# One of four weight-block sums of a gate/up stage moved from an accumulating transfer to VectorE

## The reference

```
D_FF = 5632
hn = rmsnorm(h, ffn_norm_g[i])
h = h + (jax.nn.silu(hn @ w_gate[i]) * (hn @ w_up[i])) @ w_down[i]
```

## Time and profile before

| what | value |
|---|---|
| three runs, median | 2647.73 us (2647.01 to 2650.66) |
| the profiled execution's own time | 2634.65 us |
| its span, first to last instruction | 2633.1 us |
| mean granted TensorE clock | 0.997 |
| share of the span busy: PE, DVE, ACT, POOL | 98%, 62%, 44%, 13% |
| gate/up stage | about 1074 to 1942 us of the span, 44 pairs |

### The profile page before, as it was taken

How to read it: one execution, slowest core, us unless ns; L and a number is a source line. 1 busy time by engine, 2 the same in 40 slices (tenths; PEclk the granted TensorE clock), 3 DMA queues, 4 the chain that set the end, 5 groups by cost and what they waited for, 6 DMA issues and landing times.

```text
span 2633.1 us, 43908 instructions
## 1 busy us (share of the span) xinstructions
PE 2584.3 (98%) x16270; PEld 2098.3 (80%) x16270; DVE 1620.0 (62%) x2509; ACT 1166.1 (44%) x1680; POOL 353.6 (13%) x551
## 2 busy tenths in 40 slices
PE   8999999999999999899999999999999999999998
PEld 6786777777777678788888888888887888888887
DVE  6653563663663434988989889898873333334443
ACT  6535634644644434655555555555542222233321
POOL 3000110110110100211111111111141000001100
PEclk9999999999999999999999999999999999999999
DMA  5231232132222524877777877877777445333532
GB/s 175 80 89 61 64 97 61 64 91 66 73 75 72 169 84 136 233 229 203 225 220 206 228 204 218 226 205 228 207 240 278 123 156 177 107 94 99 182 120 74
DMA packets 147813, 391.06 MB, mean 149 GB/s; under 512 B 39625, under 2 KB 43209, under 8 KB 147689
## 3 DMA queue, kind: packets, MB, share of 16 engines
q1 hardware_dynamic: 114288, 273.85, 32.8%
q0 software_dynamic: 33408, 115.62, 16.8%
HBM read 344.78 MB, written 44.63 MB: 148 GB/s over the span
## 4 chain that ended last, share of the span: by engine, by line
PE 82%; DVE 7%; DMA 4%; ACT 4%; issue 2%; SPq 1%; POOL 0%; DVEq 0%; ACTq 0%; POOLq 0%
PE bank L1419 21%; PE bank L360 15%; PE bank L357 14%; PE bank L361 14%; PE bank L1421 10%; PE bank L398 4%; DMA raw<-w_down 1%; DMA squares_scratch<-sq_x 1%; ACT w_hi L345 1%; PE bank L523 1%; DVE w_lo L352 1%; DMA raw<-w_mix 1%; PE bank L552 1%; PE bank L539 1%; DVE w_lo L1381 0%
## 5 line engine op out<-in xcount | busy, mean ns | idle before, releaser
L352 DVE TENSOR_TENSOR w_lo<-raw,w_hi 128x1024 fp32r<-128x1024 f32 (+2 forms) x308 | 330.7, 1076 | 428.4 <-ACT w_hi L345 426.9
L345 ACT ACTIVATE w_hi<-raw 128x1024 fp32r<-128x1024 f32 (+2 forms) x308 | 284.7, 926 | 516.9 <-PE bank L361 388.3
L1419 PE MATMUL bank<-x_a,w_hi 128*128 128x512 f32 x1408 | 493.0, 394 | 4.1 <-issue 2.3
L357 PE MATMUL bank<-in_hi,w_hi 128*128 128x512 f32 x1088 | 455.2, 418 | 18.7 <-DVE in_lo L2123 11.0
L360 PE MATMUL bank<-in_lo,w_hi 128*128 128x512 f32 x1088 | 440.6, 405 | 0.0
L361 PE MATMUL bank<-in_hi,w_lo 128*128 128x512 f32 x1088 | 427.8, 393 | 0.0
L1421 PE MATMUL bank<-x_a,w_lo 128*128 128x256 f32 x1408 | 390.1, 277 | 0.0
L1419 PE MATMUL bank<-x_c,w_hi 128*128 128x512 f32 x1056 | 372.9, 396 | 2.6 <-DVE x_c L1305 2.6
L1419 PEld LDWEIGHTS bank<-x_a,w_hi 128*128 128x128 f32 x1408 | 264.0, 188 | 66.7 <-issue 2.8
L1421 PE MATMUL bank<-x_c,w_lo 128*128 128x256 f32 x1056 | 293.8, 278 | 0.0
L357 PE MATMUL bank<-act_hi,w_hi 128*128 128x512 f32 x704 | 274.5, 390 | 2.1 <-DVE h_t L2194 2.1
(11 more groups left out here) (309 smaller groups left out, 3846.1 us busy)
## 6 DMA issues: line engine op xcount, KB each, us to landing
raw<-w_mix SPq DMA_DIRECT2D x116, 512.0 KB, 3.9
raw<-w_gu SPq DMA_DIRECT2D x111, 512.0 KB, 6.9
raw<-w_down SPq DMA_DIRECT2D x64, 384.0 KB, 3.1
sum<-w_gu SPq DMA_DIRECT2D x43, 512.0 KB, 5.2
sum<-w_gu POOLq DMA_DIRECT2D x43, 512.0 KB, 8.0
raw<-w_down SPq DMA_DIRECT2D x64, 320.0 KB, 2.9
raw<-ple_gate SPq DMA_DIRECT2D x32, 512.0 KB, 3.8
raw_odd<-w_gu SPq DMA_DIRECT2D x22, 512.0 KB, 6.9
```

The lines of the kernel that those rows point to most:

```text
L345: nc.scalar.activation(w_hi[:, ring_slots(par2, half), 0:cols[half]], raw[:, half, 0:cols[half]], ACT.Copy).then_inc(hi_ready, 1)
L352: nc.vector.tensor_tensor(w_lo[:, s, 0:cols[half]], raw[:, half, 0:cols[half]], w_hi[:, s, 0:cols[half]].bitcast(F32), ALU.subtract).then_ ...
L357: nc.tensor.matmul(out, w_h, x_hi, start=start, stop=False, skip_group_check=True)
L1419: nc.tensor.matmul(by_half(bank[:]), w_h, both[:, :, i, :], start=opens[j] and i == 0, stop=False, skip_group_check=True)
```

## The change

`sum_1` of pairs 2 to 43 is now a DVE instruction, added in place: SP still loads `a21` into `sum_1`, and DVE adds the `a22` that is loaded for block 6 anyway. It stands in DVE's order at the start of step 2 of the pair before, ahead of the subtract of block 6. The accumulating transfer of `sum_1` is gone from POOL, with its 512 KB of traffic; that of `sum_3` stays. SP's wait for `sum_1` of the pair before is now a wait for DVE. The counts of `sum_ready` and of the POOL semaphores are adapted.

```diff
     def sum_done(p, k):
         if isinstance(p, int) and p == 0:
             return sum_ready, k
-        if isinstance(p, int) and p == 1 and k == 1:
-            return sum_ready, 5
-        return ((S("moved_0"), SQUARES_BACK[0] + 16 * (p - 1)), (sum_ready, 2 * p + 4),
-                (S("moved_1"), SQUARES_BACK[1] + 16 * p), (sum_ready, 2 * p + 5))[k - 1]
+        return ((sum_ready, 3 * p + 2), (sum_ready, 3 * p + 3), (S("moved_1"), SQUARES_BACK[1] + 16 * p),
+                (sum_ready, 3 * p + 4))[k - 1]
...
+            if j == (3 if first else 2) and not last:
+                dve_sum(dve, p + 1, (q + 1) % QUAD, 1)
             if j == 3:
-                if first:
-                    dve_sum(dve, 1, 1, 1)
                 if not last:
                     dve_sum(dve, p + 1, (q + 1) % QUAD, 2)
...
-            nc.vector.tensor_tensor(sum_1[q % 2][:], a21 if p == 0 else sum_1[q % 2][:], a22, ALU.add
+            nc.vector.tensor_tensor(sum_1[q % 2][:], sum_1[q % 2][:] if had_one else a21, a22, ALU.add
                                     ).then_inc(sum_ready, 1)
...
-    def pool_sum_1(pool, p, q):
-        pool.wait_ge(S("x_landed_4"), 32 + 16 * p)
-        pool.dma_start(sum_1[q % 2][:], d["w_gu"][2 * p + 1][:, second_half], accum_op=ALU.add
-                       ).then_inc(S("moved_0"), 16)
...
                     pool_sum_3(pool, QUAD * i + q - 1)
-                    pool_sum_1(pool, QUAD * i + q, q)
```

More of the change, by code:

```diff
@@ L81 @@
 SQUARES_BACK = [16 + 16 * (len(range(k, KT, SQUARE_SUMS)) + 1) for k in range(SQUARE_SUMS)]
-ACTS_BACK = [SQUARES_BACK[k] + 16 * (PAIRS - 2 + k) for k in range(2)]
+ACTS_BACK = [SQUARES_BACK[0], SQUARES_BACK[1] + 16 * (PAIRS - 1)]
 DOWN_CUT_AT = (5, 8, 13)
@@ L1558, in dve_sum @@
         if k == 1:
-            if p == 0:
+            had_one = not (isinstance(p, int) and p == 0)
+            if not had_one:
                 dve.wait_ge(*landing("21", p, q))
@@ L2401, in _ @@
                 pool_sum_3(pool, t + 1)
-                pool_sum_1(pool, t + 2, t + 2)
             with pool.Fori(1, PAIRS // QUAD) as i:
```

## The result

| | kernel before | kernel after |
|---|---|---|
| median of the runs | 2648.00 us (17 runs, 2633.13 to 2650.95) | 2655.54 us (17 runs, 2652.65 to 2660.18) |
| profiled execution, its span | 2634.65, 2633.1 us | 2653.86, 2652.3 us |

The ratio is 1.0038, 95% interval 1.0025 to 1.0051: 0.38% or 7.5 us slower. The forecast was 2673.5 us (2660 to 2684), a loss of 25.8 us. The sign was right, the size was not.

The account below looks back on a forecast made before the run. PE was taken as the bound, with DVE's loop close beside it. 42 adds of 1.14 us, 47.9 us, less 22.1 us of slack left 25.8 us; 2647.7 + 25.8 = 2673.5 us, range 2660 to 2684.

Parts of the forecast that it names:

- The bound and the loop: Stage of the pairs: PE bounds at 19.41 us a pair; DVE's loop over ACT grows from 18.86 to 20.00 us.
- The 1.31 us: DVE's idle before block 3's subtract each pair, until ACT has rounded; claimed to move with DVE and absorb nothing.
- the idle before block 2: DVE's idle before block 2's subtract, 0.55 us a pair, 22.1 us over the stage; claimed to be real slack.
- 0.6 us of idle once a pair: Sign of being right: PE idles about 0.6 us before product 6, released by DVE's cu L1517.
- The slack of the loop: DVE's loop against PE's pair: 0.55 us of slack, not the 1.86 us that the idle adds up to.
- carried over, 2647.7 + 25.8: Final sum: the 25.8 us loss worked out on the profiled execution, added to the timed median, giving 2673.5 us.
- The 13.1 us: Unexplained excess of the median run over the profiled one, 2647.73 - 2634.65 us, carried over into the forecast.
- smaller loss: Rival, chance 0.12: slower PE work in the 44 pairs gives 12.5 us of further slack; time 2661.0 us.
- Transfers and SP: Removed transfers priced at nothing (bounds 0 and 13.1 us of gain); SP's moved loads have 10 us of lead, costing nothing.
- Larger loss: Rival, chance 0.07: each DVE add costs up to 1.35 us, 8.8 us more in all; time 2682.3 us.
- The price of 1.22 us: Alternative cost of each new DVE add at full duration: 51.2 us for 42, 3.4 us more than at 1.14.
- All idle is cover: Rival, chance 0.09: all 78.5 us of DVE idle before the two subtracts is slack; time stays at 2647.7 us.

Follow-up runs that it names:

- the trace of the upper group: Kernel before, unchanged, profiled once more: profiled execution 2647.54 us, 12 runs with median 2648.17 us.
- the add alone: Kernel before with one more DVE add a pair in pairs 1 to 42 (sum_2 computed twice), all transfers kept: 2655.27 us, ratio 1.0043.
- the transfer alone: Kernel before without the 42 accumulating transfers of sum_1 and nothing in their place: 2648.47 us, ratio 1.0000.
- two adds: Kernel after with a second add of the same form in step 2 of pairs 1 to 42 (sum_2 computed twice): 2708.48 us, ratio 1.0247.
- ACT rounds first: Kernel after with ACT's rounding of block 3 ahead of silu in step 6: median 2634.98 us, ratio 0.9972; a second time 2648.06 us, ratio 1.0009.
- the add over 768 columns: Kernel after with the add of sum_1 over 768 of 1024 columns in pairs 2 to 43: 2649.25 us, ratio 1.0017.

## Why the prediction was wrong in size
**The bound and the loop: right.** The 1.31 us is a detour and absorbed nothing (56.4 us before and after), the idle before block 2 is gone, PE waits for the bank before product 6, and the add costs 1.14 us. With the pitches known, 0.6 us of idle once a pair was too much to expect: PE's pair takes 19.41 or 19.79 us of the loop's 19.91.

**The slack of the loop: 0.55 us was 0.64.** The step "DVE with its detour is a loop of 19.41 - 0.55" took the idle time that the row prints. That idle counts from the printed end of the instruction before; but DVE starts an independent instruction ahead of that end. Unstalled, the subtract of block 2 starts 0.33 us after the `cg` before it (1521.47 to 1521.80 above); in the kernel before it started 0.97 us after it, at 1513.37, with a printed idle of 0.55 us:

```profile
1512.40 0.41 DVE L1520 TENSOR_TENSOR cg<-u_s,bank 128x256 f32<-128x256 f32 x1
```

0.97 - 0.33 = 0.64, the loop is 18.77 + 1.14 = 19.91 us as measured, and 42 x 0.09 = 3.8 us of the forecast cost were not there. From the first to the last of 43 subtracts of `sum_2` the kernel before takes 815.5 us (1109.59 to 1925.05) and the kernel after 837.3 (1107.10 to 1944.37): 21.8 us, where 25.8 was forecast. The spans differ by 19.2, as the profiled execution after gets to the first of these subtracts 2.5 us earlier.

**The step that failed: "carried over, 2647.7 + 25.8".** The cost was worked out on an execution with a PE pair of 19.41 us and added to a median of executions with 19.80. A bound that takes the place of another does not add to it: the time is the larger of the two, 19.91 against 19.80 there, 0.11 us a pair or 4.6 us, and somewhat more in the written-out pairs, whose loop is 20.07. In the trace of the upper group the same 42 pairs take 830.8 us (1107.47 to 1938.26), 6.5 less than in the kernel after, the spans differ by 6.3 us and the medians by 7.5. So of the 25.8 us of the forecast 4.0 were not there because of the slack, and 15.3 us (830.8 - 815.5) were already in the median to which they were added; 6.5 us remain. The 13.1 us that the prediction called unexplained were this. The rival "smaller loss" had this mechanism, slower PE work in this stage, with 0.12 of the chance and a price of 12.5 us of cover. It took 12.5 us where the traces have 15.3, and with the 4.0 us of slack that is 6.8 us less than its 2661.0; the result, 2655.5, is 5.5 less. The low end of the range was taken from it and so lay above the result.

**Transfers and SP: right.** Nothing, by the runs with the add alone and the transfer alone. SP's two loads go out at 1515.16 and 1516.25 us in the trace after, 1.1 us apart as forecast, and no new add waits for them. *Larger loss*: wrong, the add took 1.14; an add right behind the one it depends on is spaced 1.25, as the run with two adds showed. The price of 1.22 us that the prediction drew from the Trainium skill, page "VectorE: DVE Perf Modes", section "The DRAIN you can't avoid", left out that section's exception, by which a next instruction that is not held starts earlier; the spacing of 1.14 us at a duration of 1.22 fits the exception. *All idle is cover*: wrong for the order of instructions as it is, and true once ACT rounds first.

## What to carry to other kernels
Idle time of an engine is slack only if what ends it is not the engine's own earlier work: follow the releaser back until it leaves the engine or returns to it, and measure slack from start to start, against the unstalled spacing of the same two instructions. A loss worked out on one execution is a difference of two bounds; where the timed median lies off the profiled execution, first find out which stage holds the difference, as a new bound swallows it there.

## What the runs showed of the hardware
- In these traces TensorE's back-to-back pairs of matmuls (512 and 256 columns, each with its own weights, split in parts of type fp32r) run at one of two pitches, 346.6 or 353.3 ns, at a granted clock of 1.00 and 100% busy in both. It takes one when it starts after a stall and keeps it until the next, here over 2414 pairs of matmuls, 837 or 853 us. That makes 13.4 us between the medians of two groups of executions of one unchanged kernel (2635.3 and 2648.8 us, 93 executions). What decides the draw is open. In the stage with three 512-column matmuls for a block, all 13 traces agree (884 or 885 matmuls in 200 us).
- So a short stall can cost more than itself: in the kernel with the add over 768 columns the waits of PE at the fast pitch ended at the slow one, and there it stayed.
- VectorE's adds and subtracts of 128x1024 float32 take 1.22 us each and start 1.14 us apart when the second does not need the first; where it does, 1.25 us.
